# Sending the solved blocks behind the second modulation slab of the mixing

## The reference

```python
sh1, sc1, g1, sh2, sc2, g2 = modulation(c, lw)          # silu(c) @ ada_w + ada_b
h = modulate(rms_norm(x, lw["norm1_g"]), sh1, sc1)
zq, zk, zv, zqkv, zg, zb, za = jnp.split(h @ lw["w_in"], SPLITS, axis=-1)
o_na = attention(...)                                   # 8 heads, softmax
gq, gk, gv, gg, gbeta = gdn_inputs(zqkv, zb, za, lw, ...)
o_g, _ = gdn_bidirectional(gq, gk, gv, gg, gbeta, s_ctx)
x = x + g1 * (concat(o_na, gdn_output(o_g, zg, ...)) @ lw["w_out"])
x = x + g2 * hier_moe(modulate(rms_norm(x, lw["norm2_g"]), sh2, sc2), lw)
```

```python
a_mat = jnp.where(strict, jnp.einsum("bhnid,bhnjd->bhnij", kb, k) * decay, 0.0)
t_inv = lax.linalg.triangular_solve(eye + a_mat, eye, lower=True, unit_diagonal=True)
u = t_inv @ (v * beta[..., None])
w = t_inv @ (kb * jnp.exp(gc)[..., None])
```

## Time and profile before

| | us |
|---|---|
| median of 3 runs | 1226.54 (1225.91 to 1232.42) |
| profiled execution | 1225.16 |
| its span, first to last instruction | 1223.1 |
| TensorE busy | 1104.9 (90% of the span) |
| VectorE busy | 555.9 (45%) |
| mixing of layer 0, TensorE's first product with a mixing slab to its last | 214.3 to 309.2 |
| mixing of layer 1, likewise | 811.1 to 893.6 |

### The profile page before, as it was taken

The page is one execution under the profiler, slowest core; times in us unless marked ns, Lnnn a source line. Parts: engine busy times, 40 slices in busy tenths (PEclk is TensorE's granted clock), DMA queues, the critical chain, the costliest instruction groups (busy, mean ns, idle before and its releaser), DMA issues.

```text
span 1223.1 us, 18762 instructions
## 1 busy us (share of the span) xinstructions
PE 1104.9 (90%) x7521; PEld 548.7 (45%) x7521; DVE 555.9 (45%) x1416; ACT 291.9 (24%) x717; POOL 110.1 (9%) x126
## 2 busy tenths in 40 slices
PE   4899999898999999978789999989999999997776
PEld 1455544475556333322245655446745733332222
DVE  1257896466447311210162678945744742111124
ACT  0347512323122110000021672232331310100000
POOL 0020023310001000000011000242000100000001
PEclk9899999799997999999989999988999799999998
DMA  8670134967935999999983203376495399999996
GB/s 356 204 196 1 70 95 130 288 259 282 407 155 215 416 424 425 424 426 424 421 335 109 72 1 95 138 164 235 183 379 200 145 418 421 425 424 425 425 424 264
DMA packets 90794, 333.30 MB, mean 273 GB/s; under 512 B 29631, under 2 KB 32071, under 8 KB 59975
## 3 DMA queue, kind: packets, MB, share of 16 engines
q1 hardware_dynamic: 80999, 299.66, 62.7%
q0 software_dynamic: 7392, 23.93, 5.8%
q10 hardware_dynamic: 2304, 8.39, 1.7%
HBM read 314.38 MB, written 17.56 MB: 271 GB/s over the span
## 4 chain that ended last, share of the span: by engine, by line
PE 71%; SPq 11%; DMA 9%; DVE 5%; issue 2%; ACT 2%; DVEq 0%; ACTq 0%
PE bank L577 66%; SPq L1318 10%; PE bank L580 5%; DMA arena<-in_moe_w_dram 4%; DMA ring<-in_ada_w_dram 3%; DMA ring<-in_w_in_dram 2%; ACT arena L1497 2%; DVE x L1831 1%; DVE ring L1831 1%; DVE x L1823 1%; DVE arena L1823 1%; DVE small L2144 0%; DVE small L1831 0%; DVE bank L1823 0%; SPq L1407 0%
## 5 line engine op out<-in xcount | busy, mean ns | idle before, releaser
L577 PE MATMUL bank<-ring,arena 128*32 128x512 f32 (+1 forms) x2272 | 328.6, 583 | 26.4 <-issue 12.5
L577 PE MATMUL bank<-arena 128*32 128x512 f32 (+3 forms) x1600 | 267.3, 562 | 18.7 <-DMA arena<-in_moe_w_dram 10.3
L1497 ACT ACTIVATE arena<-bank 128x512 f32<-128x512 f32 (+3 forms) x292 | 124.3, 467 | 577.0 <-PE bank L580 392.5
L577 PE MATMUL bank<-ring,hT 128*128 128x512 f32 x576 | 256.9, 600 | 3.7 <-DMA ring<-in_w_in_dram 2.7
L577 PEld LDWEIGHTS bank<-ring,arena 128*32 128x32 f32 (+1 forms) x2272 | 99.0, 114 | 214.4 <-issue 212.0
L577 PEld LDWEIGHTS bank<-ring,hT 128*128 128x128 f32 x576 | 108.5, 193 | 129.5 <-issue 126.3
L577 PE MATMUL bank<-hT,ring 128*128 128x384 f32 x384 | 128.3, 488 | 0.1
L1823 DVE TENSOR_TENSOR arena<-bank,mrow 128x512 f32<-128x512 f32 x36 | 24.9, 692 | 225.2 <-PE bank L577 225.2
L577 PEld LDWEIGHTS bank<-arena 128*32 128x32 f32 (+2 forms) x1600 | 80.6, 122 | 95.1 <-issue 78.3
L577 PEld LDWEIGHTS bank<-hT,ring 128*128 128x128 f32 x384 | 71.2, 190 | 46.9 <-issue 1.3
L580 PE MATMUL bank<-const,arena 128*128 128x128 f32 x443 | 66.7, 287 | 18.2 <-DMA x<-in_x_prompt_dram 8.5
(11 more groups left out here) (162 smaller groups left out, 866.4 us busy)
## 6 DMA issues: line engine op xcount, KB each, us to landing
ring<-in_moe_w_dram SPq DMA_DIRECT2D x120, 1024.0 KB, 18.8
arena<-in_moe_w_dram SPq DMA_DIRECT2D x72, 1024.0 KB, 18.1
ring<-in_ada_w_dram SPq DMA_DIRECT2D x24, 2048.0 KB, 8.6
ring<-in_w_in_dram SPq DMA_DIRECT2D x14, 2048.0 KB, 9.7
ring<-in_w_out_dram SPq DMA_DIRECT2D x4, 2048.0 KB, 8.9
expert_dram<-arena ACTq DMA_DIRECT2D x16, 512.0 KB, 8.3
tok_dram<-arena POOLq DMA_DIRECT2D x6, 512.0 KB, 2.9
arena<-in_na_rpb_dram SPq DMA_DIRECT2D x16, 96.0 KB, 7.2
```

The costliest lines, as they stand in the source:

```text
L577: return nc.tensor.matmul(out, lhsT, rhs, start=start, stop=stop)
L1497: return nc.scalar.activation(out, in_, func, **kw)
```

## The change

In SyncE's program of each layer, `blocks_back()` is called after the load of the second mixing slab instead of before it, ahead of `state_rows()`. So SyncE's order becomes: first mixing slab; second mixing slab; `blocks_back`; `state_rows`; third mixing slab. Nothing else differs.

```diff
                 for i, name in enumerate(PRE[l]):
-                    if i == first_mixing + 1:
-                        blocks_back()
                     if l and i < len(AHEAD):
                         continue
...
                     if i == first_mixing + 1:
+                        blocks_back()
                         state_rows()
```

## The result

The changed kernel took **1242.68 us** (median of four runs, 1237.61 to 1249.4) against 1226.22 us for the kernel before (four runs, 1218.43 to 1232.42). The medians lie 16.5 us apart. The ratio of all runs is 1.0127, with a 95% interval of 1.0092 to 1.0162; by it the kernel is 15.6 us slower, 11 to 20 us. The forecast was 14.3 us. The profiled execution of the changed kernel was the longest of the four, 1249.4 us, so I profiled both kernels once more (1242.7 and 1223.98 us) and use both pairs.

What follows compares the result with a forecast made beforehand. TensorE bounds the kernel (matmuls 71% of the span), so delays count where it meets them. Layer 0's 8.8 us and layer 1's 5.5 us add 14.3 us to 1226.54 us: 1240.8 us, range 1230 to 1247 us.

Steps and rivals of the forecast that it cites:

- No gain from the second slab: Both layers' mixing: the second slab's issue stays at 214.36 and 811.18 us, set by TensorE's slot release; no gain.
- Stores, loads, blocks: Both layers' mixing: stores start 10.75 and 10.6 us later; blocks reach the pairs product 5.6 and 5.3 us late.
- the step of the blocks' landing: Mixing: from the stores' landing to the last block, GpSimd's six loads included, 6.1 us.
- the wait for VectorE behind it: TensorE, behind the pairs product: 1.04 us given back in layer 0, as much taken for layer 1.
- Rival B: Mixing: stores overtake the slab and land at 220.15 us, blocks 1.1 us late in layer 0; 1230.5 us, chance 0.13.
- Third slab, layer 0: Layer 0's mixing: third slab issued at 231.4 us, landed after 14.6 us at 246.0 us; product 7.8 us later.
- Rival D: Layer 0: third slab lands at 241.1 us, TensorE doesn't wait; total +12.1 us, 1239 us; chance 0.72 together with the forecast.
- Layer 1: the term that was mis-sized: Layer 1's mixing: 4.3 us for the blocks, 1 us clock and 0.2 us GpSimd's tail, together 5.5 us.
- TensorE's wait of 1.90 us behind GpSimd's mask: GpSimd's tail, later bias rows and mask: level in layer 0, +0.2 us in layer 1, bounds 0 and 3 us.
- Clock: TensorE's mixing: longer at the low clock, to 240 us or beyond; 1 us added per layer.
- rival C: Mixing: TensorE's idle time falls from 2.88 to some 2.3 us, low clock stretch goes; 1224 us, not slower, chance 0.05.
- Nothing given back: Rest of the mixing and the experts' stage: slots open later by the same amount, so no delay is recovered.

Runs made afterwards that it cites:

- e4_slab_scalar: The changed kernel, but ScalarE issues the second slab through its own queue at about the same time; 1241.59 us, 1.0118 times the kernel before.
- e2_layer1_only: The kernel before with the blocks sent behind the second slab in layer 1 only; 1236.87 us, 1.0075 times the kernel before.
- e1_layer0_only: The kernel before with the blocks sent behind the second slab in layer 0 only; 1238.14 us, 1.0073 times the kernel before.
- e5_stores_ahead: The changed kernel, but the blocks' four stores go ahead of the second slab and only their loads behind it; 1242.11 us, 1.0144 times the kernel before.
- e8_after_bias_first: The changed kernel, but GpSimd sends the second half of the bias rows before its wait for the blocks' stores; 1233.25 us, 1.0067 times the kernel before.
- e7_bias_first: The kernel before, but GpSimd sends the second half of the bias rows before its wait for the blocks' stores; 1219.01 us, 0.9951 times the kernel before.

## Why the prediction was right, point by point

*No gain from the second slab.* Right: it waits for TensorE's release, now as before.

*Stores, loads, blocks.* Right in size, wrong in the reason. The stores start 10.7 us later, 0.5 us behind the first slab's product instead of 10.2 us ahead of it. Loads go 9.63 and 9.80 us after the first store (10.18 and 9.78 us in the second profile); the forecast was 224.7 - 214.79 = 9.9 us. From there to the pairs product are 7.2 us instead of 6.1 us: the step of the blocks' landing was too short. The last of GpSimd's loads, now beside the state loads and the bias rows, needed up to 3.3 us where I had 2.6 us. The pairs product is 6.5 us late in both layers instead of 5.6 and 5.3 us, and the wait for VectorE behind it was given back as put. The reason for the 9.9 us was wrong: not the order within one queue, as `e4_slab_scalar` shows, but DMA engines shared between whatever is issued together. The slab and the stores together took as long as I had put them one behind the other; that the number came out is luck. Rival B, stores that overtake the slab, is out by the same rows.

*Third slab, layer 0.* Right in size: forecast landed at 246.0 us, measured 246.9 us in an execution that stands 1.4 us later. It left sooner than put, since the state loads took 1.06 us to issue and not 2.72 us, and landed after 16.0 us where I had 14.6 us; the two misses nearly cancel. Its product moved by 33.3 - 23.9 = 9.4 us instead of 7.8 us (33.1 - 23.0 = 10.1 us between the second profiles of the two kernels). In the first profile it didn't wait for the slab, against the forecast, but came 2.1 us after the landing, held up by the idle time of 3.30 us that no step of mine had. Rival D is out.

*Layer 1: the term that was mis-sized.* The sum had 5.5 us; the mixing grew by 9.7 us in the profiles and `e2_layer1_only` gives +9.2 us. Three parts make up the difference. The blocks' wait is 1.2 us longer than put. The idle time without a releaser, 1.64 us before at the same place and 3.35 us after (4.05 us in the second profile), stood in no step of mine, though its smaller form was in the trace of before. TensorE's wait of 1.90 us behind GpSimd's mask (2.42 us in the second profile) was taken at 0.2 us, with 3 us as its bound. That is 1.2 + 1.7 + 1.7 = 4.6 us for the 4.2 us that are missing, which leaves little of the 1 us that I had put down for the clock there. The last two parts vary from one execution to the next. In the profile of `e2_layer1_only` the idle time was 2.70 us, the wait behind the mask was absent, and the mixing grew by 7.1 us against the mean of the two profiles before; in `e1_layer0_only`, where layer 1 is as before, the idle time was 2.30 us.

The forecast of 1240.8 us therefore came out 1.9 us short of the median: layer 0 short by about 1 us and layer 1 by about 4 us in the profiles, while the timed runs show a smaller sum (15.6 us) than the profiles do (19.7 us). That two layers, one of them some 4 us short, came so near in the sum is partly luck.

*Clock.* The lower level did last longer (until 247 us, "240 us or beyond"), and TensorE's idle time ahead of it did fall from 2.88 to 2.25 us, which was rival C's condition. The clock fell all the same, between 220 and 222 us before and between 222 and 224 us after, so C's gain didn't come. That TensorE's rate differs between executions of one kernel (the product at 249.01 us took 1.92 us, the same one at 247.12 us in the second profile 3.64 us) says that 1 us per layer for the clock is no better than a guess of the right order.

*Nothing given back.* Right as far as can be told: between the mixings 500.7 to 503.8 us in both kernels.

## What to carry to other kernels

Before a large load is moved ahead of a small one, look at what releases it: here the slot came free at the same instant either way, and the small transfers merely lost the free time ahead of it. A store and reload through memory whose end an engine waits for belongs in such a gap; beside a 2 MB load it took 9.6 us instead of 5.4 us to its turning point, and another queue didn't help. What was to be gained here lay the other way: small loads that nobody waits for yet (the bias rows) moved into the gap saved 6 us.

## What the runs showed of the hardware

**DMA issue is held up by a large load.** Eight loads of 48 KB took SyncE 3.9 us to issue on a free queue and 8.98 to 13.54 us right behind a 2 MB slab (`e5_stores_ahead`), so an issuing engine's timeline shows the crowding, not only the landings.

**TensorE stands still with all its data there.** The idle times of 3.30, 3.35 and 4.05 us without a releaser came when the DMA engines were crowded with bias rows and a slab. DMA queues of the kernel after, 233 to 238 us and then 238 to 241 us (packets, MB, share of 16 engines):

```profile
q1 hardware_dynamic: 490, 0.96, 53.3%
q0 software_dynamic: 73, 0.17, 47.7%
...
q1 hardware_dynamic: 88, 0.72, 79.0%
q0 software_dynamic: 84, 0.17, 19.7%
q8 instruction: 1, 0.02, 2.5%
```

A queue of kind "instruction" moves one packet of 16 KB now and then, 63 in the span. In the kernel before one came 1.1 us after the start of the pairs product in each layer. In the kernel after, none came while the bias rows were issued; it came in the microsecond from 238 us, 5 us after the pairs product, and TensorE set in again at 241.02 us. In layer 1 it is the same: the packet in the microsecond from 844 us, TensorE again at 847.46 us. Two regularities hold over the mixings of all twelve profiles, in which an idle time of 1.1 us or more inside a group of like products stands 17 times. TensorE sets in again 2.4 to 2.8 us after the start of such a packet, each time. And the idle time stands at only two places of TensorE's program in each layer, always ahead of the same product; the two are 127 products apart, in layer 0 as in layer 1. I read this as TensorE waiting for its own program, whose fetch is late behind data packets. The Trainium skill (Runtime: NRT & Kernel Launch, Instruction fetch mechanics) says that an engine's instructions are refilled in blocks of 16 KiB, 256 instructions, through a DMA queue of its own, and that the cost is mostly hidden. The size agrees, and so do two numbers: TensorE's 7521 products and 7521 weight loads make 59 such blocks, and 127 products with their weight loads are 254 instructions. "Mostly hidden" doesn't hold in these places. The bias rows aren't needed for it: in layer 1 of `e8_after_bias_first` the packet came in the microsecond from 833 us and TensorE at 836.25 us, long after the bias rows had been issued, with only SyncE's loads under way. What is shown is that with the bias rows moved the idle time goes in layer 1 of `e7_bias_first` and in layer 0 of `e8_after_bias_first`, and that it stays when their packets are longer. That the packets are TensorE's program rests on these counts and times, not on a record that names the engine, and why the packet comes so late stays open.
